# A value stage with 1280 dense columns, its low-half weights on GpSimd, and the last norm's vectors loaded in eight pieces

## The chip, the core and the metric

One core of a Trainium2 chip runs the whole kernel. The metric is the device time of one execution in microseconds, from first to last instruction and what little lies around them. Engines are named as the profile names them: PE is TensorE (PEld its weight loads), DVE is VectorE, ACT is ScalarE, POOL is GpSimd, SP is SyncE, which here only issues transfers.

## The reference, cut to what matters

The program is one transformer block of one kind (convolution mixer, squared-ReLU MLP) followed by one of another (pooling and sparse attention, then a product-key expert layer). For 256 tokens of width 2048 in float32, the part that matters here is the end of the expert layer and the norm behind it:

```python
expert = jnp.take_along_axis(cidx, pos, axis=-1)        # 8 heads x 16 experts of 16384 for each token
...
v_sel = v[expert]
act = jax.nn.gelu(jnp.einsum('td,thkd->thk', xc, u_sel).astype(jnp.float32), approximate=False)
return jnp.einsum('thk,thkd->td', (gate * act).astype(x.dtype), v_sel)
...
h = layer_norm(ALPHA * h + ffn, ln2_g[l], ln2_b[l])
```

So every token sums 128 rows of the table `v` (16384 x 2048), each with its own weight, and the sum goes through the last layer norm, with a gain and a shift vector of 2048 each.

## The kernel before, in words

The weighted sum over `v` is done in two ways at once, split by columns. The first `DENSE` = 1344 columns are computed densely on TensorE: the weights of the 256 tokens are spread into a matrix over all 16384 experts (`wmat`), and the product of that matrix with `v` is accumulated over `KEYS` = 128 blocks of 128 experts each. The other `REST` = 704 columns are done sparsely: for each of the 2 x 128 slots (`t` is the half of the tokens, 128 in each) an indirect transfer fetches one row piece per token, and VectorE multiplies it by its weight and adds it up (`gathered`, in `late_pair` or `rest`). All 256 gathered slots are spread over the 128 blocks, two to each.

The dense products run in float32r, with each factor split in a high and a low half: high = rounded copy, low = value minus high. Three of the four partial products are computed (`products`): high by high, high by low, low by high. A block therefore has 2 token halves x 3 column pieces (`CUTS` = 0, 512, 1024, 1344) x 3 products = 18 matmuls, 12 of 512 columns and 6 of 320.

For block i the engines do this, in the order of their own queues:

- SP (`value_rows`, L443 to L464) loads the block's 128 x 1344 values (672 KB) into one of five slots of `v_raw`. It waits on `piece_used` until block i - 5 is done on TensorE. Eight blocks before the end of the list, at i = 120, `load_gains` puts two transfers of 128 x 2048 (1024 KB each, `gain` and `shift2`, broadcast to all partitions) into the same queue, ahead of the block's own load. They land on the part of `wmat` that belongs to blocks 0 to 63.
- ACT casts columns 0 to 1023 to `v_hi` (`value_high`), then the block's 256 weights to `g_hi` (`weights_high`), then the last columns to `v_hi`. `v_hi`, `g_hi` and `g_lo` have two buffers each. The first cast waits until TensorE has done the first two pieces of block i - 2, the weights until it has done all of it.
- VectorE does, in a fixed order, `weights_low(i)` for even i only, `gathered(2i)`, `value_low(i)` (`v_lo`, written over `v_raw`), `gathered(2i+1)`.
- POOL issues the indirect transfers (`value_row`, L567), each into one of eight row buffers, once the row eight before is used. Before every fourth row it makes the low weights of one odd block (`odd_weights_low`, L575). The order of its queue: rows 0 to 7, low weights of block 1, rows 8 to 11, low weights of block 3, and so on.
- TensorE waits for `glo_odd_ok` or `glo_ok` by the block's parity, then for `vlo_ok`, and runs the 18 matmuls (`products`, L1160 to L1182).

After the last block VectorE takes the statistics of the layer norm (`norm_stats`), waits for `gb_in` (the two vectors) and writes the output in four parts (`norm_out`).

Of the kernel before, what the change touches and what calls it, by code (L numbers as in the profile page):

```python
# [18 lines left out]
F32 = mybir.dt.float32  # L19
# [3 lines left out]
ALU = mybir.AluOpType  # L23
AX = mybir.AxisListType.X

P = 128
TOK = 256
NT = TOK // P
D = 2048
# [21 lines left out]
KEYS = 128  # L51
SLOTS = PEER_HEADS * PEER_TOPK
RING = 8
DENSE = 1344
CUTS = (0, 512, 1024, DENSE)
PIECES = len(CUTS) - 1
EARLY = CUTS[2]
REST = D - DENSE
V_SLOTS = 5
V_ROWS = 6  # L60


G_IN, G_OUT, G_MLP, G_PROJ, G_MIX, G_QRY, G_END = 0, 8, 12, 44, 54, 58, 62
# [3 lines left out]
PARTS = 4  # L67
# [29 lines left out]
def build(nc, a, out):  # L97
    with ExitStack() as ctx:
        def sem(name):
            return ctx.enter_context(nc.semaphore(name))  # L100


        def at(name, offset, shape, dtype=F32):
            return nc.alloc_sbuf_tensor_at(name, [shape[0], *shape[1:]], dtype, offset=offset)
# [145 lines left out]
        def last_use(name):  # L250
# [3 lines left out]
        wmat = at("wmat", base, [P, NT * PARTS, KEYS, PART])  # L254
        hot = at("hot", o_z, [P, 2, 2, 4, KEYS])
        v_bytes = DENSE * 4
        o_v = o_z + 64 * KB - (V_SLOTS + 1) * v_bytes
        v_hi = (at("v_hi0", o_v + V_SLOTS * v_bytes, [P, DENSE], F32R), at("v_hi1", o_z, [P, DENSE], F32R))
        g_lo = at("g_lo", o_z + v_bytes, [P, 2, NT, P], F32R)
        assert v_bytes + 2 * KB <= 8 * KB  # L260
        rest = at("rest", o_z + 8 * KB, [P, NT, REST])
        g_hi = at("g_hi", o_z + 8 * KB + NT * REST * 4, [P, 2, NT, P], F32R)
        assert 8 * KB + NT * REST * 4 <= 16 * KB - 1536 and 8 * KB + NT * REST * 4 + 2 * KB <= 16 * KB
        vrows_z = at("vrows", o_z + 16 * KB, [P, V_ROWS, REST])
        assert o_z + 16 * KB + V_ROWS * REST * 4 <= o_v and REST * 4 <= 3 * KB
        vrow = [vrows_z[:, j, :] for j in range(V_ROWS)] + [at("vrow6", o_gate, [P, REST])[:],
                                                            at("vrow7", o_c + C_END * 4, [P, REST])[:]]
        v_raw = at("v_raw", o_v, [P, V_SLOTS, DENSE])
        v_lo = at("v_lo", o_v, [P, V_SLOTS, DENSE], F32R)
        gb = (at("gain", base, [P, D]), at("shift2", base + 16 * KB, [P, D]))  # L270
# [14 lines left out]
        def sems(*names):  # L285
            return [sem(n) for n in names]
# [38 lines left out]
        zsum_ok, z_ok = sems("zsum_ok", "z_ok")  # L325
        last_diag_ok, LAST_DIAG_OK = brow_ok, HEADS
        half_ok, half_ps = n_hi["ln1"], n_op["ln1"]
        vhi_ok, vlo_ok, ghi_ok, glo_ok, piece_used, glo_odd_ok = sems(
            "vhi_ok", "vlo_ok", "ghi_ok", "glo_ok", "piece_used", "glo_odd_ok")
        v_in = part_in + [subk_in]  # L330
        alpha_ps, rest_ok, mixed_ok = sems("alpha_ps", "rest_ok", "mixed_ok")
        gb_in, var_ok, rt_ok, y_ok, y_out = sems("gb_in", "var_ok", "rt_ok", "y_ok", "y_out")

        wq_t_in, wq_z_in = poolw_in, wt_in
        gain_in, GAIN_IN = gb_in, 32
# [45 lines left out]
        def _(sp):  # L381
# [13 lines left out]
            for half in range(2):  # L395
                cols = slice(half * D // 2, (half + 1) * D // 2)
# [46 lines left out]
            def value_rows(i, slot):  # L443

                sp.dma_start(v_raw[:, slot], w_v[i]
                             ).then_inc(v_in[slot], 16)

            def load_gains():

                sp.wait_ge(glo_ok, KEYS // 4)  # L450
                sp.wait_ge(glo_odd_ok, KEYS // 4)
                for i, name in enumerate(("ln2_g", "ln2_b")):
                    sp.dma_start(gb[i][:], a[name].broadcast_to([P, D])).then_inc(gb_in, 16)

            sp.wait_ge(row_used, RING + TOK // 2 + HALF + 3 * SHARE)
            value_rows(0, 0)
# [1 line left out]
            for i in range(1, V_SLOTS):  # L458
                value_rows(i, i)
            for i in range(V_SLOTS, KEYS):  # L460
                if i == KEYS - 8:
                    load_gains()
                sp.wait_ge(piece_used, PIECES * (i - V_SLOTS + 3))
                value_rows(i, i % V_SLOTS)  # L464
            for t in range(NT):
                for half in range(2):
                    cols = slice(half * D // 2, (half + 1) * D // 2)
# [6 lines left out]
        def _(pool):  # L474
# [92 lines left out]
            def value_row(n):  # L567

                t, j, N = n // SLOTS, n % RING, NT * SLOTS // RING + n // RING
                pool.wait_ge(row_used, N * RING + (j + 1))  # L570
                pool.indirect_dma_start(vrow[j], None, a["peer_v"][0],  # L571
                                        bass.IndirectOffsetOnAxis(eid[:, t, n % SLOTS:n % SLOTS + 1], 0),
                                        element_offset=DENSE).then_inc(row_in[j], 16)

            def odd_weights_low(i):  # L575

                pool.wait_ge(ghi_ok, i + 1)
                low, high = (g[:, i % 2].rearrange("p t (q n) -> p (t q) n", q=PARTS) for g in (g_lo, g_hi))
                nc.gpsimd.tensor_tensor(low, wmat[:, :, i, :], high.bitcast(F32), ALU.subtract).then_inc(glo_odd_ok, 1)

            pool.wait_ge(row_used, RING + NT * SLOTS)
            for n in range(V_ROWS):
                value_row(n)


            pool.wait_ge(mat_ok, 2 + 2 * SLOTS // 4)
            for n in range(V_ROWS, NT * SLOTS):
                if n >= RING and n % 4 == 0:
                    odd_weights_low((n - RING) // 2 + 1)
                value_row(n)  # L590
            for i in (KEYS - 3, KEYS - 1):
                odd_weights_low(i)


        @block.tensor
        def _(pe):
# [563 lines left out]
            def products(i, c, t, stop=False):  # L1160

                cols = slice(CUTS[c], CUTS[c + 1])
                vh, vl = v_hi[i % 2][:, cols], v_lo[:, i % V_SLOTS, cols]
                dst = acc[t][c][:, 0:CUTS[c + 1] - CUTS[c]]
                gh, gl = g_hi[:, i % 2, t, :], g_lo[:, i % 2, t, :]
                nc.tensor.matmul(dst, gh, vh, start=False, stop=False)  # L1166
                nc.tensor.matmul(dst, gh, vl, start=False, stop=False)  # L1167
                return nc.tensor.matmul(dst, gl, vh, start=False, stop=stop)  # L1168

            for i in range(KEYS):  # L1170
                pe.wait_ge(glo_odd_ok if i % 2 else glo_ok, i // 2 + 1)
                pe.wait_ge(vlo_ok, i + 1)
                if i < KEYS - 1:
                    for c in range(PIECES):
                        for t in range(NT):
                            last = products(i, c, t)
                        last.then_inc(piece_used, 1)
                    continue
                for t in range(NT):
                    for c in range(PIECES):  # L1180
                        products(i, c, t, stop=True).then_inc(mixed_ok, 1)
# [570 lines left out]
        def _(dve):  # L1752
            step = Steps(dve, dve_step)
            V = nc.vector
# [81 lines left out]
            for half in range(2):  # L1836
                cols = slice(half * D // 2, (half + 1) * D // 2)
# [498 lines left out]
            def value_low(i):  # L2336

                dve.wait_ge(vhi_ok, 2 * i + 2)
                V.tensor_tensor(v_lo[:, i % V_SLOTS], v_raw[:, i % V_SLOTS], v_hi[i % 2][:].bitcast(F32),
                                ALU.subtract).then_inc(vlo_ok, 1)  # L2340

            def weights_low(i):

                dve.wait_ge(ghi_ok, i + 1)
                V.tensor_tensor(g_lo[:, i % 2].rearrange("p t (q n) -> p (t q) n", q=PARTS), wmat[:, :, i, :],
                                g_hi[:, i % 2].bitcast(F32).rearrange("p t (q n) -> p (t q) n", q=PARTS),
                                ALU.subtract).then_inc(glo_ok, 1)

            def gathered(n):

                j, N, t = n % RING, NT * rounds + n // RING, n // SLOTS
                dve.wait_ge(row_in[j], 16 * N + 16)
                dve.wait_ge(row_used, N * RING + (RING + j))
                before = rest[:, t, :] if n % SLOTS == 0 else rest_sum
                after = rest[:, t, :] if n % SLOTS == SLOTS - 1 else rest_sum
                V.scalar_tensor_tensor(after, vrow[j], coef[:, t, n % SLOTS:n % SLOTS + 1],
                                       before, ALU.mult, ALU.add).then_inc(row_used, 1)
# [62 lines left out]
            dve.wait_ge(coefT_ok, 2 + PARTS)  # L2420

            for i in range(KEYS):
                if i % 2 == 0:
                    weights_low(i)
                gathered(2 * i)
                if i:
                    value_low(i)
                gathered(2 * i + 1)
# [27 lines left out]
            dve.wait_ge(row_used, (NT + 2) * (SLOTS // RING) * RING + RING)  # L2456
            norm_stats(0)
            norm_stats(1)
            dve.wait_ge(gb_in, GAIN_IN + 32)
            for t in range(NT):  # L2460
                for half in range(2):
                    norm_out(t, half)
# [54 lines left out]
```

## Time and profile before

| | us |
|---|---|
| median of 3 runs | 2696.4 (2694.79 to 2696.91) |
| the profiled execution, its own time | 2694.49 |
| its span, first to last instruction | 2692.7 |
| value stage, first to last dense matmul | about 2194.6 to 2676.0 |
| mean granted TensorE clock over the span | 0.919 |

The whole of the value stage and the norm is the last fifth of the span. Times in the rows below are microseconds from the start of the span. Busy times are those of the engine in the stretch named; the share of DMA is that of the core's 16 DMA engines, and GB/s what they moved.

### The profile page before, as it was taken

The page shows a single profiled execution, that of the slowest core. Times are in us where ns is not written, and L with a number is a line of the kernel's source. Part 1 is how long each engine was busy: PE and PEld are TensorE (multiplying, and loading weights), DVE is VectorE, ACT ScalarE, POOL GpSimd, SP SyncE. Part 2 cuts the span into 40 slices and gives each one's busy share as a digit, 9 for nine tenths or more (in the row PEclk, how much of TensorE's full clock was granted, in tenths as well). Part 3 has the DMA queues.
Part 4 walks back from the last instruction along what each step waited for, and adds up shares of the span by engine and source line. Part 5 has one row for each costly group of instructions (what it writes and reads, how often), then busy time and mean ns, then how long its engine had stood idle before and what let it go on. Part 6 is the DMA issues. An engine that isn't in the chain of part 4 may idle for free. (4 is left out here: it accounts for less than half of the span.)

```text
span 2692.7 us, 39987 instructions
## 1 busy us (share of the span) xinstructions
PE 2352.6 (87%) x14075; PEld 2094.1 (78%) x14075; DVE 1901.7 (71%) x2885; ACT 1299.2 (48%) x2277; POOL 1964.1 (73%) x1065
## 2 busy tenths in 40 slices
PE   7998999999999999999999878882334479999996
PEld 7997888888888888999988767882322368888885
DVE  4998653623514417456515999989999789999997
ACT  4455455454454455343443013337997844444442
POOL 4887888888888887778783566777787646666663
PEclk9999999999999999999999988895555589999998
DMA  7552555555555554555454999999999959999996
GB/s 234 173 173 94 187 172 189 188 184 188 187 187 187 187 187 158 174 195 173 157 172 172 414 399 392 417 421 422 389 422 422 368 210 391 384 381 382 382 384 242
DMA packets 231587, 722.94 MB, mean 268 GB/s; under 512 B 17388, under 2 KB 53796, under 8 KB 198304
## 3 DMA queue, kind: packets, MB, share of 16 engines
q1 hardware_dynamic: 168416, 356.03, 38.5%
q0 software_dynamic: 57344, 360.74, 33.5%
q10 hardware_dynamic: 5696, 4.47, 0.5%
q8 instruction: 76, 1.25, 0.2%
q14 instruction: 55, 0.45, 0.0%
HBM read 717.51 MB, written 3.67 MB: 268 GB/s over the span
## 5 line engine op out<-in xcount | busy, mean ns | idle before, releaser
L479 POOL TENSOR_TENSOR w_lo<-raw,w_hi 128x1024 fp32r<-128x1024 f32 x464 | 1130.6, 2457 | 251.3 <-ACT w_hi L1196 249.4
L1196 ACT CAST w_hi<-raw 128x1024 fp32r<-128x1024 f32 x464 | 483.9, 1050 | 619.7 <-PE bank L615 407.6
L613 PE MATMUL bank<-B,w_hi 128*128 128x512 f32 x1280 | 457.1, 402 | 13.5 <-DVE B L1794 9.7
L613 PE MATMUL bank<-A,w_hi 128*128 128x512 f32 x1280 | 450.3, 397 | 1.4 <-DVE A L1807 1.4
L615 PE MATMUL bank<-B,w_lo 128*128 128x256 f32 x1280 | 361.3, 282 | 0.0
L615 PE MATMUL bank<-A,w_lo 128*128 128x256 f32 x1280 | 358.8, 280 | 0.0
L1939 DVE TENSOR_TENSOR sq<-bank,T 128x256 f32<-128x256 f32 x128 | 54.1, 425 | 411.9 <-ACT T L1392 411.6
L618 PE MATMUL bank<-A,w_hi 128*128 128x256 f32 x1152 | 331.1, 287 | 6.1 <-DVE A L1844 2.6
L619 PE MATMUL bank<-A,w_hi 128*128 128x256 f32 x1152 | 327.8, 285 | 0.0
L620 PE MATMUL bank<-A,w_lo 128*128 128x256 f32 x1152 | 327.7, 284 | 0.0
L1666 ACT CAST v_hi<-v_raw 128x1024 fp32r<-128x1024 f32 (+1 forms) x256 | 192.3, 751 | 258.1 <-PE bank L1168 249.1
L613 PEld LDWEIGHTS bank<-B,w_hi 128*128 128x128 f32 x1280 | 242.4, 189 | 75.7 <-issue 10.1
L1094 PE MATMUL late_pair<-hot 128*128 128x128 f32 x512 | 119.6, 408 | 200.4 <-ACT hot L1608 187.3
L613 PEld LDWEIGHTS bank<-A,w_hi 128*128 128x128 f32 x1280 | 240.4, 188 | 59.8 <-POOL w_lo L479 1.7
L538 POOL DMA_INDIRECT rows_split<-in_peer_u,eid x96 | 186.2, 1939 | 131.7 <-DVE dots L2260 55.7
L1094 PEld LDWEIGHTS late_pair<-hot 128*128 128x128 f32 x512 | 103.1, 300 | 217.3 <-issue 209.0
L571 POOL DMA_INDIRECT vrows<-in_peer_v,eid x192 | 205.1, 1068 | 61.3 <-issue 29.4
L615 PEld LDWEIGHTS bank<-B,w_lo 128*128 128x128 f32 x1280 | 244.0, 191 | 0.0
L615 PEld LDWEIGHTS bank<-A,w_lo 128*128 128x128 f32 x1280 | 242.1, 189 | 0.0
L618 PEld LDWEIGHTS bank<-A,w_hi 128*128 128x128 f32 x1152 | 222.5, 193 | 9.3 <-issue 8.8
L619 PEld LDWEIGHTS bank<-A,w_hi 128*128 128x128 f32 x1152 | 222.5, 193 | 0.3
L620 PEld LDWEIGHTS bank<-A,w_lo 128*128 128x128 f32 x1152 | 222.7, 193 | 0.0
(390 smaller groups left out, 5198.8 us busy)
## 6 DMA issues: line engine op xcount, KB each, us to landing
raw<-in_mlp_w SPq DMA_DIRECT2D x128, 1024.0 KB, 5.1
v_raw<-in_peer_v SPq DMA_DIRECT2D x128, 672.0 KB, 7.6
raw<-in_w_in SPq DMA_DIRECT2D x40, 1024.0 KB, 5.0
raw<-in_cc_w_in SPq DMA_DIRECT2D x64, 512.0 KB, 4.7
raw<-in_cc_w_out SPq DMA_DIRECT2D x16, 1024.0 KB, 5.0
raw<-in_w_out SPq DMA_DIRECT2D x16, 1024.0 KB, 5.1
raw<-in_peer_wq SPq DMA_DIRECT2D x8, 1024.0 KB, 11.2
wq_t<-in_peer_wq SPq DMA_DIRECT2D x2, 2048.0 KB, 24.4
```

What stands on the lines that cost most here:

```text
L479: nc.gpsimd.tensor_tensor(w_lo[:, s % 4], raw[:, s // 2, 2 * (s % 2):2 * (s % 2) + 2, :], w_hi[:, s % 4].bitcast(F32), ALU.subtract).then_ ...
L538: pool.indirect_dma_start(row(t, j), None, a["peer_u"][0], bass.IndirectOffsetOnAxis(eid[:, t, slot:slot + 1], 0)).then_inc(row_in[j], 16)
L571: pool.indirect_dma_start(vrow[j], None, a["peer_v"][0], bass.IndirectOffsetOnAxis(eid[:, t, n % SLOTS:n % SLOTS + 1], 0), element_offset= ...
L613: nc.tensor.matmul(bank[m][:].rearrange("p (s t) -> p s t", s=2), wh, both[:, :, kt, :], start=(kt == 0), stop=False)
L615: last = nc.tensor.matmul(bank[m][:, TOK:2 * TOK], wl, hi[:, kt, :], start=False, stop=(kt == KT - 1))
L618: nc.tensor.matmul(dst, wh, hi[:, kt, :], start=(kt == 0), stop=False)
L619: nc.tensor.matmul(dst, wh, lo[:, kt, :], start=False, stop=False)
L620: last = nc.tensor.matmul(dst, wl, hi[:, kt, :], start=False, stop=(kt == KT - 1))
L1094: last = nc.tensor.matmul(misc[2 + h][:, i * P:(i + 1) * P], hot[:, h, 1, i, :], hot[:, h, 0, i, :], start=True, stop=True)
L1196: nc.scalar.copy(w_hi[:, s % 4], raw[:, s // 2, 2 * (s % 2):2 * (s % 2) + 2, :]).then_inc(hi_done, 1)
L1666: nc.scalar.copy(v_hi[i % 2][:, cols], v_raw[:, i % V_SLOTS, cols]).then_inc(vhi_ok, 1)
L1939: V.tensor_tensor(sq[:, m, :], bank[m][:, 0:TOK], fold[:, m, :], ALU.add).then_inc(bank_free[m], 1)
```

## The change

Four edits, all in the value stage.

1. `DENSE` becomes 1280 and `REST` 768. The third piece of a block has 256 columns in place of 320, a dense load 128 x 1280 values (640 KB), a gathered row 768 values (3072 B in place of 2816 B).
2. `weights_low` leaves VectorE. POOL makes the low weights of every block: those of blocks 0 and 1 before row 8, and from then on one block's before every second row.
3. TensorE waits on one semaphore, `glo_ok`, for every block.
4. The two broadcast loads of 1024 KB at i = 120 become eight of 128 x 512 (256 KB each) at i = 76, 81, ..., 111, gain and shift in turn. Before the first, SP waits until the low weights of 64 blocks are made.

```diff
-DENSE = 1344
+DENSE = 1280
...
+GAIN_FROM, GAIN_LOADS = 76, 8
...
-            def load_gains():
-
-                sp.wait_ge(glo_ok, KEYS // 4)
-                sp.wait_ge(glo_odd_ok, KEYS // 4)
-                for i, name in enumerate(("ln2_g", "ln2_b")):
-                    sp.dma_start(gb[i][:], a[name].broadcast_to([P, D])).then_inc(gb_in, 16)
+            def gain_columns(n):
+
+                cols = slice(n // 2 * 512, n // 2 * 512 + 512)
+                name = ("ln2_g", "ln2_b")[n % 2]
+                sp.dma_start(gb[n % 2][:, cols], a[name][:, cols].broadcast_to([P, 512])).then_inc(gb_in, 16)
...
             for i in range(V_SLOTS, KEYS):
-                if i == KEYS - 8:
-                    load_gains()
+                if i == GAIN_FROM:
+                    sp.wait_ge(glo_ok, KEYS // 2)
+                if i >= GAIN_FROM and (i - GAIN_FROM) % 5 == 0 and i < GAIN_FROM + 5 * GAIN_LOADS:
+                    gain_columns((i - GAIN_FROM) // 5)
                 sp.wait_ge(piece_used, PIECES * (i - V_SLOTS + 3))
                 value_rows(i, i % V_SLOTS)
...
-            def odd_weights_low(i):
+            def weights_low(i):
 
                 pool.wait_ge(ghi_ok, i + 1)
                 low, high = (g[:, i % 2].rearrange("p t (q n) -> p (t q) n", q=PARTS) for g in (g_lo, g_hi))
-                nc.gpsimd.tensor_tensor(low, wmat[:, :, i, :], high.bitcast(F32), ALU.subtract).then_inc(glo_odd_ok, 1)
+                nc.gpsimd.tensor_tensor(low, wmat[:, :, i, :], high.bitcast(F32), ALU.subtract).then_inc(glo_ok, 1)
...
             for n in range(V_ROWS, NT * SLOTS):
-                if n >= RING and n % 4 == 0:
-                    odd_weights_low((n - RING) // 2 + 1)
+                if n == RING:
+                    weights_low(0)
+                if n >= RING and n % 2 == 0:
+                    weights_low((n - RING) // 2 + 1)
                 value_row(n)
-            for i in (KEYS - 3, KEYS - 1):
-                odd_weights_low(i)
+            for i in range(KEYS - 3, KEYS):
+                weights_low(i)
...
-                pe.wait_ge(glo_odd_ok if i % 2 else glo_ok, i // 2 + 1)
+                pe.wait_ge(glo_ok, i + 1)
...
             for i in range(KEYS):
-                if i % 2 == 0:
-                    weights_low(i)
                 gathered(2 * i)
...
-            dve.wait_ge(gb_in, GAIN_IN + 32)
+            dve.wait_ge(gb_in, GAIN_IN + 16 * GAIN_LOADS)
```

## Rows read from the trace of the kernel before

**Rows 1.** The page: busy time of each engine; bytes moved per slice of 67.3 us.
```profile
PE 2352.6 (87%) x14075; PEld 2094.1 (78%) x14075; DVE 1901.7 (71%) x2885; ACT 1299.2 (48%) x2277; POOL 1964.1 (73%) x1065
...
GB/s 234 173 173 94 187 172 189 188 184 188 187 187 187 187 187 158 174 195 173 157 172 172 414 399 392 417 421 422 389 422 422 368 210 391 384 381 382 382 384 242
```

**Rows 2.** Waits in 2300 to 2600 us: waiter, releaser: us in total, times, longest.
```profile
ACT v_hi L1666 <- PE bank L1168: 159.9, 81, 2.2
```

**Rows 3.** Windows of the value stage: busy of each engine, clock, DMA share, GB/s.
```profile
2225.00:2240.00 15.00, 15.00 (x75) 12.68 (x74) 14.04 (x15) 7.00 (x13) 9.99 (x10) 1.00 1.02 405
...
2300.00:2600.00 300.00, 300.00 (x1465) 254.72 (x1464) 280.87 (x286) 139.18 (x244) 198.32 (x205) 1.00 1.00 383
2620.00:2640.00 20.00, 18.64 (x92) 15.67 (x91) 14.34 (x15) 6.93 (x13) 11.84 (x13) 1.00 1.01 407
```

**Rows 4.** Line L445 (dense block loads): time from issue to landing.
```profile
DMA to landing us min/median/max: 4.4/7.6/15.5
```

**Rows 5.** Line L571 (gathered rows): time from issue to landing.
```profile
DMA to landing us min/median/max: 3.8/7.5/10.3
```

**Rows 6.** Timeline, TensorE, two blocks: start, us, line, output<-inputs, sizes.
```profile
2402.51 0.47 PE L1166 MATMUL bank<-v_hi,g_hi 128*128 128x512 f32 x1
...
2406.21 0.39 PE L1166 MATMUL bank<-v_hi,g_hi 128*128 128x512 f32 x1
...
2408.95 0.31 PE L1166 MATMUL misc<-v_hi,g_hi 128*128 128x320 f32 x1
2409.10 0.31 PE L1167 MATMUL misc<-v_lo,g_hi 128*128 128x320 f32 x1
...
2409.88 0.47 PE L1166 MATMUL bank<-v_hi,g_hi 128*128 128x512 f32 x1
```

**Rows 7.** Timeline, VectorE, the same two blocks: idle before and its releaser in brackets.
```profile
2406.98 0.43 DVE L2345 TENSOR_TENSOR g_lo<-wmat,g_hi 128x256 fp32r<-128x256 f32 x1 [0.35 <-ACT g_hi L1671]
2407.32 0.95 DVE L2356 SCALAR_TENSOR_TENSOR late_pair<-vrows,coef,late_pair 128x704 f32<-128x704 f32 x1
2408.18 1.55 DVE L2339 TENSOR_TENSOR v_lo<-v_raw,v_hi 128x1344 fp32r<-128x1344 f32 x1
2409.65 0.95 DVE L2356 SCALAR_TENSOR_TENSOR late_pair<-vrows,coef,late_pair 128x704 f32<-128x704 f32 x1
2410.70 0.96 DVE L2356 SCALAR_TENSOR_TENSOR late_pair<-vrow,coef,late_pair 128x704 f32<-128x704 f32 x1
```

**Rows 8.** Timeline, VectorE, around the loads of the last norm's vectors.
```profile
2613.51 0.42 DVE L2345 TENSOR_TENSOR g_lo<-wmat,g_hi 128x256 fp32r<-128x256 f32 x1 [0.36 <-ACT g_hi L1671]
...
2640.82 0.42 DVE L2345 TENSOR_TENSOR g_lo<-wmat,g_hi 128x256 fp32r<-128x256 f32 x1 [5.54 <-ACT g_hi L1671]
...
2665.61 0.43 DVE L2345 TENSOR_TENSOR g_lo<-wmat,g_hi 128x256 fp32r<-128x256 f32 x1 [0.37 <-ACT g_hi L1671]
```

**Rows 9.** Timeline, TensorE, another stage: sixteen 256-column products in a row, first and last.
```profile
1119.85 0.28 PE L618 MATMUL bank<-A,w_hi 128*128 128x256 f32 x1
...
1121.65 0.28 PE L618 MATMUL bank<-A,w_hi 128*128 128x256 f32 x1
```

**Rows 10.** Line L1964, VectorE, an earlier stage, both inputs in SBUF: ns min/median/max.
```profile
L1964 DVE TENSOR_TENSOR X<-sq,X x64: 410/2615/2633, 474.1 to 1093.3; 128x256 f32<-128x256 f32 x64
```

**Rows 11.** Timeline, GpSimd, the same two blocks.
```profile
2403.28 0.74 POOL L579 TENSOR_TENSOR g_lo<-wmat,g_hi 128x256 fp32r<-128x256 f32 x1 [1.58 <-ACT g_hi L1671]
2404.17 0.96 POOL L571 DMA_INDIRECT vrows<-in_peer_v,eid  x1
...
2410.64 0.74 POOL L579 TENSOR_TENSOR g_lo<-wmat,g_hi 128x256 fp32r<-128x256 f32 x1 [1.56 <-ACT g_hi L1671]
```

**Rows 12.** Timeline, all engines, the stage's start.
```profile
2194.59 0.50 PE L1166 MATMUL bank<-v_hi,g_hi 128*128 128x512 f32 x1 [0.94 <-DVE g_lo L2345]
...
2196.24 0.73 POOL L579 TENSOR_TENSOR g_lo<-wmat,g_hi 128x256 fp32r<-128x256 f32 x1
```

**Rows 13.** Line L479, GpSimd, the same stage and others: ns min/median/max.
```profile
L479 POOL TENSOR_TENSOR w_lo<-raw,w_hi x464: 2340/2404/4460, 18.3 to 1429.1; 128x1024 fp32r<-128x1024 f32 x155
```

More of the change, by code:

```diff
@@ L327, in build @@
         half_ok, half_ps = n_hi["ln1"], n_op["ln1"]
-        vhi_ok, vlo_ok, ghi_ok, glo_ok, piece_used, glo_odd_ok = sems(
-            "vhi_ok", "vlo_ok", "ghi_ok", "glo_ok", "piece_used", "glo_odd_ok")
+        vhi_ok, vlo_ok, ghi_ok, glo_ok, piece_used = sems(
+            "vhi_ok", "vlo_ok", "ghi_ok", "glo_ok", "piece_used")
         v_in = part_in + [subk_in]
@@ L2340, in value_low @@
                                 ALU.subtract).then_inc(vlo_ok, 1)
[L2342 to L2347, printed above, removed]
             def gathered(n):
```

## The prediction, made from the rows above

> **What bounds the kernel now.** I read the page first: the last seven slices hold the value stage, and there the transfers run at 381 to 391 GB/s, where the row gathers before it reach 422 [rows 1]. The change touches only this stage, so the question is which of its engines sets the pace of a block. The waits say that ACT, which makes the high halves, waited for TensorE 81 times between 2300 and 2600 us, once a block, and never for a load [rows 2]. The windows agree: PE is busy 300 of 300 us at the full clock (1.00, the 2.4 GHz level), while DMA also shows a share of 1.00 at 383 GB/s [rows 3]. A share of 1.00 with nobody waiting is not yet a bound; it says that transfers are always outstanding. A dense load lands after 7.6 us and a gathered row after 7.5 us [rows 4, 5]. The load of block i is issued when block i - 5 ends, and ACT wants it 2.75 blocks, some 10 us, later. So some 2.5 us of slack is left.
>
> The pace itself is in the timeline of TensorE: two blocks from 2402.51 to 2409.88 are 7.37 us, 3.685 a block [rows 6]. Twelve 512-column products take 2408.95 - 2406.21 = 2.74 us (0.228 each), a 320-column one 0.146 (2408.95 to 2409.10). That makes 2.74 + 6 x 0.146 = 3.62; the other 0.07 are short waits at each block's start. VectorE stands close behind: in the same two blocks it idles only 0.35 us, before `g_lo` [rows 7].
>
> One stall stands out. The two loads of the last norm's vectors go ahead of block 120, and VectorE's `g_lo` then waits 5.54 us. From 2613.51 to 2665.61 lie six pairs of blocks in 52.10 us [rows 8]; at 7.37 they would take 44.2. The stall costs **7.9 us**.
>
> **TensorE after.** The 256-column product is in the trace: sixteen from 1119.85 to 1121.65 stand 1.80 / 15 = 0.120 us apart, with the same 128 x 128 weights changed for each [rows 9]. A block becomes 2.74 + 6 x 0.120 = 3.46 us.
>
> **VectorE after.** It loses `g_lo` (0.34 a pair, from 2406.98 to 2407.32). Its steps in one block are gather to `v_lo` 0.86, `v_lo` to gather 1.47, gather to gather 1.05 [rows 7]. Per column a two-input subtraction costs (1552 - 410) / (1344 - 256) = 1.05 ns, from `v_lo` at 1.55 us and the shortest 256-column one [rows 7, 10]; 64 columns are 0.07. One `v_lo` gets shorter and two gathers longer: 0.93 + 1.40 + 1.12 = 3.45 us a block. That is no more than TensorE needs.
>
> **GpSimd after.** One cycle of its queue (low weights, four row issues) lasts 2410.64 - 2403.28 = 7.36 us, of which 1.56 are a wait for `g_hi`; the low weights cost it 0.89 (to 2404.17) [rows 11]. A second one makes 7.36 - 1.56 + 0.89 = 6.69, or 3.35 us a block. Behind the waiting low weights stand the row issues, and behind those VectorE: row 2b + 6 is issued some 1.7 us into block b - 1 and wanted before `v_lo` of block b + 3, about 10 us later; it lands after 7.5. Every second block's issues come about 0.9 us later than now. That is covered, with some 2 us over.
>
> **Transfers after.** A block now moves 128 x 1344 x 4 + 2 x 128 x 704 x 4 = 1.409 MB, which at 3.685 us is the 383 GB/s seen. It will move 0.655 + 0.786 = 1.442 MB. The best stretch with this traffic alone is 405 GB/s for 15 us, and 407 with the vectors in it [rows 3]; both show a full queue, so I take 405: 1.442 / 0.405 = **3.56 us a block**. That is above 3.46: the transfers become the bound. The ends: at the 422 of the 8 KB row gathers [rows 1] it is 3.42 and TensorE stays the bound at 3.46; at 383, if that is already the limit, 3.76.
>
> The bound does not bite at once. The five slots are full at the start, and each block at 3.46 runs the transfers 0.10 us further behind. The 2.5 us of slack last 25 blocks. So 25 blocks gain 3.685 - 3.46 = 0.225 (5.6 us) and some 102 gain 0.125 (12.8 us).
>
> **The vectors.** The stall goes: -7.9. Spread in eight pieces of 256 KB, each delays the block load behind it in SP's queue by 0.65 us. In a stage bound by transfers these add in full: 2.10 MB / 405 GB/s = +5.2; with TensorE as the bound the slack hides them. SP's new wait costs nothing: at i = 76 it has already waited for block 73.
>
> **The start.** Now VectorE makes the low weights of block 0 and TensorE starts at 2194.59. GpSimd first has rows 6 and 7 to issue and comes free at 2196.24 [rows 12]. Then block 0 takes 0.73: TensorE starts at about 2197.0, **+2.4**.
>
> Merging two semaphores costs nothing. The norm's tail works on the same 2048 columns in as many instructions: nothing. The wider `rest` and narrower start of the sums are made beside the expert rows' transfers; uncovered it would be under 0.2 us.
>
> **Sum.** -5.6 - 12.8 - 7.9 + 5.2 + 2.4 = -18.7 us. Against the profiled execution's 2694.5 that is 2675.8; the median of the runs lies 1.9 above that execution, so I predict **2678**. With the transfer rate between 400 and 412 and the pieces half hidden, this case spans 2670 to 2686.
>
> **Rivals.**
> - *The transfers keep up* (3.46 to 3.50 a block). For it: single slices above 420 [rows 1]. Against: no long stretch of this mix above 405. Then 127 x 0.2 = -25.4, -7.9, +2.4: 2665.
> - *383 GB/s is already the limit* (slower). For it: share 1.00. Then 3.76: 125 x 0.08 = +9.9, vectors +5.5, -7.9, +2.4: 2706. It decides from 3.685 a block on, that is below 391 GB/s. Against: the 405 and 407 stretches.
>
> The Trainium skill ("DMA: Bandwidth & Descriptors", Specifications) gives an HBM limit of about 358 GB/s for a core; by it a block would take 4.03 us and the present one 3.94. The measured 383 and 422 contradict that here.
> - *GpSimd and VectorE collide.* Low weights and `v_lo` are both subtractions with two inputs in SBUF. In an earlier stage such a 256-column one on VectorE took 410 ns at best but 2615 in the median, beside GpSimd's subtractions of 2404 [rows 10, 13]: one waits for the other's whole instruction. Today the two lie apart, since GpSimd's 0.74 us falls beside a gather [rows 7, 11]. With one low weight in every block, `v_lo` may be asked for while it runs (up to 0.35 us of waiting, behind ACT's last cast), or, if GpSimd is late, GpSimd waits for all 1.4 us of `v_lo`. Its 3.35 becomes up to 4.75 in such a block, and the rows behind it come late. If that sets in often, I estimate 3.62 to 3.75 a block: -8 to +8, with -7.9 and +2.4: 2683 to 2699, middle 2690. Against: after ACT's `g_hi` GpSimd comes first by the order of ACT's queue, and catches up 0.1 to 0.2 us a block.
>
> The Trainium skill ("SBUF — State Buffer", SBUF: two separate sides) has this as an exclusive lock on a shared pair of ports, held for a whole instruction by whoever starts first. By this rule the wait in the likely order is 0.35 us and is covered; in the other order this rival holds.
>
> **Chances.** Forecast 0.50, transfers keep up 0.18, collision 0.22, limit already reached 0.10. The range 2663 to 2696 leaves out most of the last and the ends of the others. A measurement of this kernel tells 0.2% (5.4 us) from no change. Faster than that: forecast, keep up and half the collision, 0.78. Same: 0.12. Slower: 0.10, nearly all from the limit.
>
> **What would show it.** In the changed profile: windows between 2300 and 2600 with GB/s above 400 and PE slightly below full; ACT's `v_hi` waiting for the load and no longer for PE (forecast), or still for PE (first rival); the 256-column products 0.12 apart; `v_lo` still near 1.49 us, longer if the two engines collide; POOL's waits for `g_hi` nearly gone; landing times up to 9 or 10 us; no stall after 2620; TensorE's start 2.4 us later. The prediction is wrong above all if the rate with both queues full is not near 405, or if small idle gaps let TensorE's granted clock fall from 1.00.

## The result, and the profile after

| | before | after |
|---|---|---|
| median, us | 2695.9 (4 runs, 2694.79 to 2696.91) | 2723.6 (4 runs, 2717.69 to 2733.56) |
| profiled execution | 2694.49 | 2733.56 |
| first gather of the value stage starts | 2194.5 | 2202.0 |
| last gather of the value stage starts | 2671.7 | 2710.7 |
| between the two | 477.2 | 508.7 |

The kernel became **slower**: ratio 1.012, 95% interval 1.0091 to 1.015. Forecast were 2678 us and a range up to 2696. The value stage alone grew by 31.5 us. The later start, 7.5 us, isn't put down to the change: in the traces of this study the stage starts anywhere from 2184.9 to 2203.6, and the instructions before it are the same but for a few widths (that of `rest`, and of the first block's); the kernels with 704 gathered columns alone start from 2187.7 to 2201.6. Below, therefore, the stage's own length (first to last gather in the trace) stands beside each median. It is that of one execution, the profiled one; the changed kernel's was the longest of its four.

In the slices of the value stage the page has 363 to 374 GB/s where the forecast had more than 400, and POOL is busier (2092.4 us, before 1964.1):

```profile
PE 2355.3 (86%) x14075; PEld 2080.7 (76%) x14075; DVE 1906.5 (70%) x2821; ACT 1293.1 (47%) x2277; POOL 2092.4 (77%) x1129
...
GB/s 231 170 174 98 178 168 186 188 179 196 175 184 197 176 192 169 164 201 170 132 194 218 412 384 408 416 421 392 416 422 387 357 231 364 364 363 370 374 372 252
```

The window and the waits from 2300 to 2600 (waiter, releaser: us in total, times, longest) answer to [rows 2, 3]:

```profile
2300.00:2600.00 300.00, 279.85 (x1358) 227.89 (x1357) 258.86 (x227) 124.56 (x226) 263.84 (x226) 1.00 0.98 368
```

```profile
ACT v_hi L1670 <- PE bank L1172: 176.9, 76, 2.8
PEld bank L1170 <- POOL g_lo L581: 33.6, 67, 0.9
DVE v_lo L2343 <- ACT v_hi L1670: 28.5, 57, 0.9
...
PE bank L1170 <- POOL g_lo L581: 18.7, 44, 0.7
```

TensorE has gaps (280 of 300 us busy), and they end with GpSimd's `g_lo`: 0.4 to 0.5 us in the mean, 0.9 at most. ACT still waits for TensorE and never for a load. So the transfers, at less than 370 GB/s, are not the bound. GpSimd is: the chain of waits from 2401 to 2410 lies wholly in its queue, on its row issues, its low weights and the gaps between them (whole pieces are counted against the 9 us, so the shares add up to more than 100%):

```profile
by line: POOL vrows L573 71.5%; POOL g_lo L581 24.9%; issue 12.5%
```

How the loop closes is seen in the four timelines, where [rows 6, 7, 11] showed the same engines before. TensorE (a block starts at 2401.49, the one two later at 2409.41):

```profile
2401.49 0.50 PE L1170 MATMUL bank<-v_hi,g_hi 128*128 128x512 f32 x1 [0.36 <-POOL g_lo L581]
...
2404.34 0.28 PE L1170 MATMUL misc<-v_hi,g_hi 128*128 128x256 f32 x1
2404.45 0.28 PE L1171 MATMUL misc<-v_lo,g_hi 128*128 128x256 f32 x1
...
2409.41 0.50 PE L1170 MATMUL bank<-v_hi,g_hi 128*128 128x512 f32 x1 [0.34 <-POOL g_lo L581]
```

ACT, the casts for the block after next:

```profile
2404.60 1.05 ACT L1670 CAST v_hi<-v_raw 128x1024 fp32r<-128x1024 f32 x1 [2.42 <-PE bank L1172]
2405.55 0.40 ACT L1675 CAST g_hi<-wmat 128x256 fp32r<-128x256 f32 x1
2405.85 0.40 ACT L1670 CAST v_hi<-v_raw 128x256 fp32r<-128x256 f32 x1
```

VectorE, two `v_lo`:

```profile
2402.21 1.49 DVE L2343 TENSOR_TENSOR v_lo<-v_raw,v_hi 128x1280 fp32r<-128x1280 f32 x1 [0.29 <-ACT v_hi L1670]
...
2406.29 1.49 DVE L2343 TENSOR_TENSOR v_lo<-v_raw,v_hi 128x1280 fp32r<-128x1280 f32 x1 [0.53 <-ACT v_hi L1670]
```

GpSimd:

```profile
2402.87 1.65 POOL L573 DMA_INDIRECT vrows<-in_peer_v,eid  x1 [0.30 <-issue]
2404.54 0.75 POOL L581 TENSOR_TENSOR g_lo<-wmat,g_hi 128x256 fp32r<-128x256 f32 x1
2405.45 0.97 POOL L573 DMA_INDIRECT vrows<-in_peer_v,eid  x1 [0.16 <-issue]
2406.73 1.87 POOL L573 DMA_INDIRECT vrows<-in_peer_v,eid  x1 [0.30 <-issue]
2408.61 0.75 POOL L581 TENSOR_TENSOR g_lo<-wmat,g_hi 128x256 fp32r<-128x256 f32 x1
```

Read them as one chain. TensorE starts a block at 2401.49; ACT's first cast for the block after next starts when its twelfth product is through, 2404.60, and the last one at 2405.85. VectorE's `v_lo` for it runs from 2406.29 to 2407.78. GpSimd has begun a row issue at 2406.73, beside that `v_lo`, and it takes 1.87 us instead of 0.95: it ends at 2408.60, **0.82 us after `v_lo`**. The one before began at 2402.87, beside the `v_lo` that ended at 2403.70, and ended at 2404.52, again 0.82 after. Behind the issue in GpSimd's queue stand the low weights (2408.61), and behind these TensorE, 2409.41. Two blocks take 7.92 us, 3.96 each (3.99 in the mean from 2300 to 2600), and the next round is the same.

The whole trace shows this picture. Of the stage's 250 row issues 124 take more than 1.03 us, up to 2.26, and each of these ends 0.81 to 0.85 us after a VectorE instruction with two inputs in SBUF. From 2300 to 2600 row issues spend 64 us above 0.95 each, which is 0.86 us a block; in the kernel before it was 13 us. The low weights are seldom caught: 3 of 128 take more than 0.8 us.

Two details came out as forecast: the 256-column products stand 0.11 to 0.12 us apart (2404.34, 2404.45), and the vectors in pieces cause no stall. From issue to landing they take

```profile
DMA to landing us min/median/max: 6.5/8.0/10.7
```

### The profile page after: what moved, and what is told of

It reads as the page before. It is cut to its first block and busy times, and to the rows that moved or that the text cites. A ratio compares the mean times of both kernels' runs of the same rounds, so it can differ in the third digit from the quotient of the medians.

```text
span 2731.7 us, 39991 instructions
## 1 busy us (share of the span) xinstructions
PE 2355.3 (86%) x14075; PEld 2080.7 (76%) x14075; DVE 1906.5 (70%) x2821; ACT 1293.1 (47%) x2277; POOL 2092.4 (77%) x1129
## 5 line engine op out<-in xcount | busy, mean ns | idle before, releaser
L1670 ACT CAST v_hi<-v_raw 128x1024 fp32r<-128x1024 f32 (+1 forms) x256 | 185.3, 724 | 296.5 <-PE bank L1172 296.5
L573 POOL DMA_INDIRECT vrows<-in_peer_v,eid x192 | 260.4, 1356 | 60.0 <-issue 42.8
L617 PEld LDWEIGHTS bank<-A,w_hi 128*128 128x128 f32 x1280 | 241.0, 188 | 63.2 <-DVE X L1934 2.9
L1170 PE MATMUL bank<-v_hi,g_hi 128*128 128x512 f32 x512 | 214.7, 419 | 36.2 <-POOL g_lo L581 34.4
L619 PEld LDWEIGHTS bank<-A,w_lo 128*128 128x128 f32 x1280 | 242.5, 189 | 0.0
L622 PEld LDWEIGHTS bank<-A,w_hi 128*128 128x128 f32 x1152 | 222.4, 193 | 9.4 <-issue 8.9
L2343 DVE TENSOR_TENSOR v_lo<-v_raw,v_hi 128x1280 fp32r<-128x1280 f32 x128 | 192.1, 1501 | 50.0 <-ACT v_hi L1670 49.2
```

The source lines that it names most:

```text
L573: pool.indirect_dma_start(vrow[j], None, a["peer_v"][0], bass.IndirectOffsetOnAxis(eid[:, t, n % SLOTS:n % SLOTS + 1], 0), element_offset= ...
L617: nc.tensor.matmul(bank[m][:].rearrange("p (s t) -> p s t", s=2), wh, both[:, :, kt, :], start=(kt == 0), stop=False)
L619: last = nc.tensor.matmul(bank[m][:, TOK:2 * TOK], wl, hi[:, kt, :], start=False, stop=(kt == KT - 1))
L622: nc.tensor.matmul(dst, wh, hi[:, kt, :], start=(kt == 0), stop=False)
```

## The experiments

**Every low weight on GpSimd, nothing else** (e1). The changed kernel with 1344 columns and both vectors at block 120.

```diff
-DENSE = 1280
+DENSE = 1344
...
-                if i >= GAIN_FROM and (i - GAIN_FROM) % 5 == 0 and i < GAIN_FROM + 5 * GAIN_LOADS:
-                    gain_columns((i - GAIN_FROM) // 5)
+                if i == KEYS - 8:
+                    load_gains()
```

> The kernel before, with one edit of the four alone: GpSimd makes the low weights of every block (1344 dense columns, both vectors loaded at block 120). Theory A, read from the changed trace: a row issue on GpSimd that starts while VectorE's v_lo (two inputs in SBUF) runs is held until v_lo ends, and stands in front of the next low weights, on which TensorE waits. The loop over two blocks is then 2.85 (TensorE's first twelve products) + 0.26 + 1.26 + 0.45 (ACT's casts) + 0.03 + 1.55 (v_lo) + 0.82 (rest of the row issue) + 0.02 + 0.75 (low weights) + 0.05 = 8.04 us, 4.02 a block: about 2735 us. Theory B, the extra bytes of 1280 columns are what costs: this kernel has none of them, so 2685 to 2700.

2738.7 us, ratio 1.0156 (1.0131 to 1.0181); stage 515.4 us. Theory A's loop of 4.02 us a block is there (4.03 in the mean from 2300 to 2600). The row issue ends 0.82 us after `v_lo` (GpSimd, then VectorE):

```profile
2403.73 1.80 POOL L570 DMA_INDIRECT vrows<-in_peer_v,eid  x1 [0.30 <-issue]
2405.53 0.76 POOL L578 TENSOR_TENSOR g_lo<-wmat,g_hi 128x256 fp32r<-128x256 f32 x1
```

```profile
2403.15 1.56 DVE L2340 TENSOR_TENSOR v_lo<-v_raw,v_hi 128x1344 fp32r<-128x1344 f32 x1 [0.51 <-ACT v_hi L1667]
```

This one edit (with the single semaphore that belongs to it) carries the whole loss. It needs neither the 1280 columns nor the pieces.

**That edit undone** (e2). 1280 columns and pieces, but VectorE makes the low weights of even blocks.

```diff
...
             for i in range(KEYS):
+                if i % 2 == 0:
+                    weights_low(i)
                 gathered(2 * i)
```

> The changed kernel with one edit undone: VectorE makes the low weights of the even blocks again; 1280 columns and the eight pieces stay. Theory A: the loop through GpSimd is gone; VectorE's steps are 7.14 to 7.4 us a pair of blocks, the stall at the vectors is gone: 2678 to 2692 us. Theory B: the transfers hold it at 3.9 us a block, as in the changed kernel: 2715 or more.

2689.3 us, ratio 0.9991 (0.9972 to 1.0011); stage 468.6. Theory A holds, B falls.

**The pieces alone** (e3), on the kernel before.

```diff
-                if i == KEYS - 8:
-                    load_gains()
...
+                if i >= GAIN_FROM and (i - GAIN_FROM) % 5 == 0 and i < GAIN_FROM + 5 * GAIN_LOADS:
+                    gain_columns((i - GAIN_FROM) // 5)
```

> The kernel before, with one edit alone: the vectors in eight pieces. The prediction's term for it, where transfers have slack: the stall of 7.9 us goes and nothing else moves: 2688 us. Rival: each piece pushes the block load behind it by 0.65 us and ACT waits for it eight times: 2690 to 2693.

2689.3 us, ratio 0.9971 (0.9956 to 0.9986); stage 469.2 us, 8.0 less than before, where the term was 7.9 (one trace of each; the medians of this round lie 5.7 apart). The rival's waits of ACT for loads are absent. Beside it e2 shows that 1280 columns without the move of the low weights are worth nothing measurable (468.6). The traces say why: with `g_lo` still in its queue VectorE stands idle for only 13.5 of 300 us in e2, TensorE waits 38 times for `v_lo`, and a block takes 3.69 us in both.

**`v_lo` with one input in SBUF** (e4), on the changed kernel. It takes a fixed PSUM value from v in place of its high half.

```diff
-                V.tensor_tensor(v_lo[:, i % V_SLOTS], v_raw[:, i % V_SLOTS], v_hi[i % 2][:].bitcast(F32),
+                V.tensor_tensor(v_lo[:, i % V_SLOTS], v_raw[:, i % V_SLOTS], late_pair[:, 1023:1024].broadcast_to([P, DENSE]),
```

> The changed kernel, where v_lo subtracts one fixed PSUM value, read 1280 times, and not v_hi: the same instruction over the same columns with one input in SBUF. This leaves the right low halves of v out of the computation; transfers, waits and order are the same. Theory A (row issues wait for v_lo's second SBUF input): the long row issues of 1.6 to 2.0 us become 0.95, the block falls from 3.95 to 3.5 to 3.6 us: 2665 to 2685 us. Theory B, or a slow row issue for another reason (DMA rings full): the row issues stay long and the time near 2720.

2674.2 us, ratio 0.9928 (0.9902 to 0.9955); stage 461.4. The second row issue behind the low weights now takes 0.95 us. In the whole stage 124 issues begin inside a `v_lo` with over 0.2 us of it left, and none of them takes more than 0.98:

```profile
2402.97 0.75 POOL L581 TENSOR_TENSOR g_lo<-wmat,g_hi 128x256 fp32r<-128x256 f32 x1 [0.46 <-issue]
2403.86 0.97 POOL L573 DMA_INDIRECT vrows<-in_peer_v,eid  x1
2405.14 0.95 POOL L573 DMA_INDIRECT vrows<-in_peer_v,eid  x1 [0.30 <-issue]
```

And with the hold gone the forecast's picture appears: 407 GB/s over 200 us, and ACT waiting for the load.

```profile
2300.00:2500.00 200.00, 196.25 (x999) 166.57 (x998) 186.36 (x168) 92.15 (x168) 147.31 (x167) 1.00 1.02 407
```

```profile
ACT v_hi L1670 <- DMA v_raw<-in_peer_v: 51.3, 23, 4.2
```

This run separates the two halves of the prediction. Same bytes, same queues, `v_lo` 1.48 us where it was 1.49; only the second SBUF input is missing, and 49 us of the median and 47 of the stage go. It frees the low weights too, but in the changed kernel these were caught only 3 times in 128, so nearly all of it is the row issues.

The new input is also one value read 1280 times, and that could matter by itself. The traces answer this without another run. The gathers `late_pair<-vrows,coef,late_pair` read as many different PSUM values as they have columns; in the fourteen traces 890 row issues begin inside such a gather with over 0.2 us of it left, and none takes more than 1.03. And the first gather of each half of the tokens starts from `rest`, so that both of its large inputs lie in SBUF. It holds a row issue even in e4 and e8. In e8 (VectorE, then GpSimd) the issue ends 0.81 us after it:

```profile
2198.07 0.95 DVE L2356 SCALAR_TENSOR_TENSOR late_pair<-vrows,coef,rest 128x704 f32<-128x704 f32 x1
```

```profile
2198.39 1.44 POOL L571 DMA_INDIRECT vrow<-in_peer_v,eid  x1 [0.31 <-issue]
```

So it is the second SBUF input that holds the issue, not the kind of instruction and not the repeated value. In the fourteen traces together 1164 row issues begin more than 0.05 us into an instruction with two SBUF inputs (`v_lo`, or such a gather), with over 0.2 us of it left, and every one of them ends 0.81 to 0.85 us after it.

**The low weights one row earlier** (e5).

```diff
...
-                if n == RING:
+                if n == V_ROWS:
                     weights_low(0)
-                if n >= RING and n % 2 == 0:
-                    weights_low((n - RING) // 2 + 1)
+                if n % 2 == 1:
+                    weights_low((n - V_ROWS + 1) // 2)
...
```

> The changed kernel with GpSimd's low weights one row earlier in its queue: those of block b before row 2b+5, not 2b+6, so blocks 0 and 1 come before rows 6 and 7. Theory A: in the queue two row issues still stand between one block's low weights and the next, and the second is still held by v_lo, so the pace stays at 3.95 us a block; only the start comes 2.3 us earlier: 2717 to 2723 us. Theory C, what costs is the place of the low weights or that the rows come late: the time moves by 10 us or more either way.

A miss: 2739.5 us, ratio 1.0176 (1.014 to 1.0212); stage 523.0. Two costs that I had at nothing. The rows come too late, so VectorE waits for them; and now the low weights themselves are caught (45 of 128 take more than 0.8 us), 2.05 us in place of 0.74, in turn with a row issue of 2.26.

```profile
DVE late_pair L2353 <- DMA vrows<-in_peer_v,eid: 30.8, 40, 2.1
```

```profile
2402.50 2.26 POOL L573 DMA_INDIRECT vrows<-in_peer_v,eid  x1 [0.30 <-issue]
...
2407.91 2.05 POOL L581 TENSOR_TENSOR g_lo<-wmat,g_hi 128x256 fp32r<-128x256 f32 x1
```

**`v_lo` in two halves, a gather between** (e6).

```diff
-                    value_low(i)
-                gathered(2 * i + 1)
+                    value_low_half(i, 0)
+                gathered(2 * i + 1)
+                if i:
+                    value_low_half(i, 1)
```

> The changed kernel with v_lo made by two instructions of 640 columns, the second gather between them. Computation the same. Theory A: a row issue that starts beside v_lo is now held for 0.8 us at most, and a gather with one SBUF input follows, so the loop through GpSimd shortens by 0.6 to 0.75 us a block, to the transfers' 3.55: 2670 to 2690 us. VectorE pays 0.07 us a block. If GpSimd's slow issues have another cause, the time stays at 2720 or rises by the 9 us of extra instructions.

Missed: 2697.7 us, ratio 1.0015 (0.9997 to 1.0034), 26 us less than the changed kernel but above the 2670 to 2690 expected. The stage is 486.7 in the profiled execution, which was the longest of the ten (2708.8). The holds are short now, no issue takes more than 1.43 us, but one of the two halves is held as well, by GpSimd's low weights: 1.43 us for 640 columns beside 0.81. In that execution VectorE has become the bound: it is busy 297.8 of the 300 us from 2300 to 2600.

```profile
2403.57 1.43 DVE L2345 TENSOR_TENSOR v_lo<-v_raw,v_hi 128x640 fp32r<-128x640 f32 x1
...
2405.85 0.81 DVE L2345 TENSOR_TENSOR v_lo<-v_raw,v_hi 128x640 fp32r<-128x640 f32 x1
```

**The same halves, adjacent** (e7).

```diff
...
             def value_low(i):
 
-                dve.wait_ge(vhi_ok, 2 * i + 2)
...
+                value_low_half(i, 0)
+                value_low_half(i, 1)
```

> The changed kernel with v_lo made by two instructions of 640 columns with nothing between them. Theory A leaves one thing open: whether GpSimd gets in between the two. If it does, as in the kernel with a gather between: 2675 to 2695. If the second half follows too closely, the row issue is held through both, and the time stays at 2715 to 2730.

Median 2696.7, but the ten executions lie from 2678.4 to 2733.4; the ratio, 0.9998 (0.9964 to 1.0031), leaves out the two longest, 2724.4 and 2733.4. The profiled one (2681.1, stage 461.8) is in a good rhythm: one row issue of two is held, by 0.4 us, and a turn of GpSimd's queue takes 3.55 us, just what the transfers need. In it GpSimd does get in between the halves: the first half ends at 2405.16, the second runs to 2405.90, and the row issue begun at 2404.63 ends at 2406.00, 0.84 after the first.

```profile
2403.72 0.75 POOL L582 TENSOR_TENSOR g_lo<-wmat,g_hi 128x256 fp32r<-128x256 f32 x1
2404.63 1.37 POOL L574 DMA_INDIRECT vrows<-in_peer_v,eid  x1 [0.16 <-DVE late_pair L2360]
2406.31 0.95 POOL L574 DMA_INDIRECT vrows<-in_peer_v,eid  x1 [0.30 <-issue]
2407.27 0.75 POOL L582 TENSOR_TENSOR g_lo<-wmat,g_hi 128x256 fp32r<-128x256 f32 x1
```

The long ones, up to 2733, were not profiled; that they fall into the loop of the changed kernel is a guess and not shown.

**One input on the kernel before** (e8): the edit of e4.

> The kernel before, where v_lo subtracts one fixed PSUM value and not v_hi, as in the fourth run: one input in SBUF, the right low halves of v are left out of the computation. Theory A: the one row issue in four that took 1.14 us falls to 0.95, GpSimd's waits for g_hi grow by 0.2 us a pair, and the time does not move beyond run to run differences, since GpSimd is not what sets the pace there: 2683 to 2700 us.

One run, 2698.6 us; stage 477.7 against 477.2. All four row issues take 0.95 to 0.97, and GpSimd's wait for `g_hi` grows from 1.56 to 1.75:

```profile
2400.33 0.97 POOL L571 DMA_INDIRECT vrows<-in_peer_v,eid  x1
2401.61 0.95 POOL L571 DMA_INDIRECT vrows<-in_peer_v,eid  x1 [0.30 <-issue]
2402.86 0.95 POOL L571 DMA_INDIRECT vrow<-in_peer_v,eid  x1 [0.30 <-issue]
2404.12 0.95 POOL L571 DMA_INDIRECT vrow<-in_peer_v,eid  x1 [0.30 <-issue]
2406.82 0.74 POOL L579 TENSOR_TENSOR g_lo<-wmat,g_hi 128x256 fp32r<-128x256 f32 x1 [1.75 <-ACT g_hi L1671]
```

In the kernel before, one of them took 1.15. It began inside a `v_lo` and ended 0.83 us after it, while the one that began just before a `v_lo` took 0.95 (GpSimd, then VectorE):

```profile
2405.44 1.15 POOL L571 DMA_INDIRECT vrows<-in_peer_v,eid  x1 [0.30 <-issue]
...
2408.14 0.95 POOL L571 DMA_INDIRECT vrows<-in_peer_v,eid  x1 [0.30 <-issue]
```

```profile
2404.20 1.56 DVE L2339 TENSOR_TENSOR v_lo<-v_raw,v_hi 128x1344 fp32r<-128x1344 f32 x1
```

So the hold was there before, mostly 0.2 us per pair of blocks, hidden in GpSimd's wait of 1.56: 71 issues of the stage begin inside a `v_lo` with over 0.2 us of it left, and all 71 take 1.13 us or more. In e8 there are 64 of them, and none takes more than 0.97.

**Every fourth block's low weights on VectorE** (e9; with 1344 columns e11; with 1312 e12; with the two halves e10).

```diff
...
             def weights_low(i):
 
+                if i % 4 == 0:
+                    return
...
             for i in range(KEYS):
+                if i % 4 == 0:
+                    weights_low(i)
                 gathered(2 * i)
...
```

> The changed kernel (1280 columns, eight pieces), but VectorE makes the low weights of every fourth block, 0 included, and GpSimd the other three. GpSimd's queue needs 3.35 - 0.22 = 3.13 us a block and has 0.4 left for being held, VectorE's 3.45 + 0.09 = 3.54. Theory A: the loop through GpSimd is broken once in four blocks and can't lock in; the transfers set 3.55 us a block and the start costs nothing: 2668 to 2685 us. If one block without GpSimd is too little, the loop holds in the other three: 2690 to 2715.

> Every fourth block's low weights on VectorE, eight pieces, and 1344 dense columns as in the kernel before. TensorE needs 3.62 us a block, VectorE 3.39 + 0.09 = 3.48, the transfers 1.409 MB / 405 = 3.48: TensorE sets the pace with both others clear of it: 2680 to 2690 us, where the pieces alone gave 2689. If GpSimd's holds bind here too: above 2695.

> The same with 1312 dense columns. TensorE 2.74 + 6 x 0.133 = 3.54, transfers 1.425 MB / 405 = 3.52, VectorE 3.42 + 0.09 = 3.51: all three at 3.5 to 3.55, so 2666 to 2682 us if they stay apart, and no faster than 1280 columns if the nearness of three engines costs waits.

> As the run before, and v_lo in two adjacent instructions of 640 columns. Shorter holds, but VectorE needs 3.54 + 0.10 = 3.64 us a block and becomes the bound: 2680 to 2695 us, with less spread than the two halves alone (2678 to 2733).

e9: 2714.0 us, ratio 1.0079 (1.0051 to 1.0106), stage 502.5. e11: 2720.4, 1.01 (1.0071 to 1.013), 504.9. e12: 2718.9, 1.0092 (1.0059 to 1.0124), 501.9. The main expectation missed in all three, whatever the columns, and the alternative named with each holds: 0.4 us of room a block on GpSimd is too little. Row issues and low weights are caught in turn (e9):

```profile
2407.43 1.99 POOL L574 DMA_INDIRECT vrow<-in_peer_v,eid  x1 [0.30 <-DVE late_pair L2366]
...
2410.69 2.05 POOL L584 TENSOR_TENSOR g_lo<-wmat,g_hi 128x256 fp32r<-128x256 f32 x1
...
2414.16 2.27 POOL L574 DMA_INDIRECT vrows<-in_peer_v,eid  x1 [0.30 <-issue]
```

e10: 2685.9 us, ratio 0.9964 (0.9945 to 0.9983), stage 464.1, executions from 2672.9 to 2690.1. As expected: a block takes 3.65 us, where 3.64 were worked out for VectorE, and VectorE is busy 194 of 200 us. With short holds GpSimd waits for `g_hi` again, so it keeps up, and the transfers reach 400 GB/s:

```profile
POOL g_lo L585 <- ACT g_hi L1682: 24.6, 41, 1.6
```

```profile
2300.00:2500.00 200.00, 197.41 (x996) 166.73 (x995) 193.97 (x236) 91.67 (x166) 158.40 (x152) 1.00 1.01 400
```

By median it is the fastest version that computes everything; its interval overlaps that of the pieces alone.

## Why the prediction was wrong

**The step that failed** is "GpSimd after": "7.36 - 1.56 + 0.89 = 6.69, or 3.35 us a block". The sum took the row issues at the length they had in one rhythm. Their length is not a constant: an issue that begins while VectorE runs a subtraction with two SBUF inputs ends 0.82 us after that one. With GpSimd's slack gone, one issue of two meets `v_lo` and takes 1.2 to 2.3 us, 1.8 in the mean. A turn of GpSimd's queue without holds is 3.13 us (0.74 + 0.15 + 0.97 + 0.30 + 0.95 + 0.02, the lengths and gaps in the traces), so the 3.35 was even high; the holds add 0.86, and a block takes 3.98 over the stage (508.7 us less the start). Shown by e4 and e8: where the second SBUF input is taken away, every issue but two in each is back at 0.94 to 0.98, and these two begin beside the gather that still has two inputs in SBUF.

The row was at hand: the 1.15 us issue of the kernel before, which ends 0.83 after `v_lo`, one of 72 held in that trace. I read GpSimd's rows by the whole turn and not one by one against VectorE's.

**The collision rival** had the mechanism and the wrong partners. It named low weights against `v_lo`, and judged from the order of ACT's queue that these come first. In the changed kernel they mostly do (75 of them with a mean of 0.75 us from 2300 to 2600). It did not name the row issues, which are two of three of GpSimd's instructions. It also had no loop: I priced a hold as a cost to GpSimd alone, while the held issue stands ahead of the low weights that TensorE needs, and TensorE's delay sets the next `v_lo`. Hence 2723.6, where it ended at 2699. The Trainium skill ("SBUF — State Buffer", § SBUF: two separate sides) says that a VectorE instruction with two SBUF inputs and a GpSimd instruction that reads SBUF share a port pair, and that the one that starts first has it to its end. The traces agree for the low weights (2.05 for 0.74 and 1.43 for 0.81, each the one that came second) and show the same for indirect row issues.

**TensorE, VectorE, the vectors and the start** came out: 0.12 us a product; gathers 1.02 and `v_lo` 1.49; the stall of 7.9 us, shown alone by e3 (8.0). In the changed trace TensorE starts 3.46 us after ACT's first `g_hi` begins (2201.20, 2204.66), before it was 1.30 (2193.29, 2194.59): +2.2 where +2.4 was forecast. One small term was dropped: the 3.46 us a block leave out the 0.07 of short waits that are in the 3.685 with which they are compared.

**Transfers** were right where they could be seen: 405 GB/s forecast, 407 in e4, whose stage is 15.8 us shorter than before against the 18.7 forecast. That e4's median, 2674.2, falls even below 2678 is in part luck: two of its four executions, the profiled one with them, lie near 2669, and that one starts its stage at 2184.9, the earliest of all. In the changed kernel they never became the bound, so the 5.2 us for the vectors were not paid there. The forecast is short by 50 us of stage: 127 blocks at 3.98 in place of some 3.54 are +56, less those 5.

**The rival of a limit at 383 GB/s** is excluded by e4. The slower outcome, given 0.10, came by another way.

Open: why e7's executions spread over 55 us, and whether another order of GpSimd's queue holds with every low weight there. e5 shows only that one row earlier doesn't.

## What to carry to other kernels

Before work is moved to GpSimd, lay its instructions one by one against VectorE's two-input ones: a length measured while it had slack says nothing about its length without. In this kernel 0.78 us of free time a block (1.56 a pair, before) kept the holds hidden and 0.4 (e9, e11, e12) did not; where the border lies no run shows. With 0.4 it took shorter holding instructions as well (e10). And look at what stands behind the held instruction in its queue: a hold costs little until something that the bounding engine needs is queued behind it.

## What the runs showed of the hardware that I had not expected

- An indirect row issue on GpSimd (0.95 us alone) that begins during a VectorE instruction with both large inputs in SBUF, a subtraction or the gather that reads `rest`, ends 0.81 to 0.85 us after it, 1164 times of 1164 in the traces here. With one of the inputs in PSUM it isn't held (e4, e8, and the other gathers everywhere), nor if it begins 0.04 us ahead of the subtraction (2408.14 and 2408.18 in the kernel before).
- The hold goes both ways for the low weights: 2.05 us for 0.74 on GpSimd if `v_lo` is first (e5), 1.43 for 0.81 on VectorE if they are (e6).
- Dense block loads and gathers of 3 KB rows together run at 406 GB/s over the 300 us from 2300 to 2600 (e4).
- The work ahead of the stage, the same but for a few widths, ends 18.7 us apart between the profiled executions (2184.9 to 2203.6), which is more than many of the effects measured here.
